# Where three chunks of modulation products run: in the delta scan, or behind the first feed-forward layer in another bank

## The chip, the cores and the metric

One Trainium2 chip, one core. The metric is the time of one execution on the device in microseconds (us). Engines: TensorE (PE, matmuls; PEld its weight loads), VectorE (DVE), ScalarE (ACT), GpSimd (POOL) and SyncE (SP, which issues nearly all loads).

## What is computed

A stack of two blocks on 256 tokens of width 1024, batch 1, all in float32. The first block has two layers: a hybrid mixer (gated delta rule and attention) with a feed-forward layer, then a conformer convolution with a feed-forward layer. The second block (`second_block`) follows on its output. What matters here is the modulation of the first block's layers:

```python
def ada_terms(cond, w_mod, b_mod):
    m = jax.nn.silu(cond) @ w_mod + b_mod          # (D,) @ (D, 6 D)
    return jnp.split(m, 6, axis=-1)

for layer in range(DEPTH):                          # DEPTH = 2
    sh1, sc1, gt1, sh2, sc2, gt2 = ada_terms(c[:, None, :], w_mod[layer], b_mod[layer])
    a = modulate(rms_norm(h, g_mix_pre[layer]), sh1, sc1)
    ...
    h = h + gt1 * rms_norm(y, g_mix_post[layer])
    f = swiglu_ffn(modulate(rms_norm(h, g_ffn_pre[layer]), sh2, sc2), w_ffn_in[layer], w_ffn_out[layer])
    h = h + gt2 * rms_norm(f, g_ffn_post[layer])
```

Layer 1's six vectors are needed at different times: the first three (shift, scale, gate of the mixer) around the conformer, the last three (shift, scale, gate of the feed-forward) only after the conformer.

## The kernel before

Every weight goes through a ring of four slots of 3072 columns in SBUF. `ORDERED` lists all chunks in the order of their use; `SLOT_OF` gives the slot, `BEFORE` the chunk that a load has to wait for, `DONE` the semaphore and count that tell that a chunk is used. SP walks this list in order: wait until the chunk's slot is free, issue the load, next. A load that has to wait holds back all that follow.

**Modulation.** `w_mod` of each layer is cut into 16 chunks of 384 output columns (1536 KB each), `MODS` lists all 32. `mod_products(m)` (its matmuls are L815) does 8 matmuls of 128x384 for one chunk, in four column groups of PE; the page counts each of them twice (x16). They accumulate in `mod_acc`, part of PSUM bank 7, over a whole run of chunks. `MOD_RUNS` has three runs: chunks 0 to 5, 6 to 15 (both layer 0) and 16 to 31 (layer 1). At the end of a run ACT copies `mod_acc` to SBUF (L1790), PE turns it into columns with the selection matrix (`mod_columns`, L823, into `mod_out`, also bank 7), DVE adds the bias (`mod_take`, L2248) and `mod(layer, vectors)` makes gains, shifts and the columns `pcol` of the post-norms.

**The delta scan.** It has four steps of short dependent matmuls (L1109, `per_head`) with DVE work between them. To fill the time PE has generators of other work and a table `GAPS`, written out by hand: at each named place of the scan (`pause(name)`) every letter advances one generator: M one chunk of modulation products, S attention scores (L1179), T transposes of attention weights (L776), V attention outputs (L1200), N the normalisation of weights (ACT and DVE only). ACT and DVE walk the same table with their own generators, so the letters set the order on three engines. `SLOT_OF` uses three of the four slots there. Chunks 6 to 31 all run in the scan or just ahead of it; then the four chunks of the mixer's output projection (`hyb_o`) follow, split into a high and a low part by ACT (L1985) and DVE (L2619), and `out_rows_parts` (L905) multiplies them into banks 4 to 7 (`Y`: token tile 0 in banks 4 and 5, tile 1 in 6 and 7). It waits until DVE has read the scan's last banks (L2689).

**The first feed-forward layer** (`ffn("ffn0", ...)`) runs 22 blocks: input products (L955, L956), then row products (L990) into `Y`. At its end the rows of tile 0 are finished before those of tile 1. `post(1)` (DVE L2342 to L2350, ACT L1674 to L1683) normalises and adds to `h`, `norm_stats(3)` and `norm_scale(3)` make the next norm, PE transposes it (`norm(3)`, 16 transposes, L789), ACT (L1636) and DVE (L2300) apply gain and shift.

**The conformer.** `glu_pair(c)` (L832) makes value and gate of one block of 128 features from one `conf_i` chunk (1024 KB); ACT reads the gate (L2048), DVE the value (L2735). Eight pairs, then the convolution: `conv_taps`, which writes banks 4 to 7, and `conv_sum`.

```python
GAPS = {
...
    "ds1": "SMTM", "ks2": "VMNM", "vn2": "SMTM", "os2": "MNS", "ds2": "TMNM", "oi2": "SMVM", "ks3": "TMNM", "vn3": "MTM",
    "os3": "MV",
}
MOD_RUNS = ((0, MOD_CTX), (MOD_CTX, NMOD), (NMOD, NMODS))
```

Of the kernel before, what the change touches and what calls it, by code (L numbers as in the profile page):

```python
# [25 lines left out]
ALU = mybir.AluOpType  # L26
ACT = mybir.ActivationFunctionType
# [3 lines left out]
P = 128  # L31
# [27 lines left out]
MOD_C = 384  # L59
# [20 lines left out]
MODS = [("mod0", _j) for _j in range(NMOD)] + [("mod1", _j) for _j in range(NMOD)]  # L80
ORDERED = MODS[:MOD_CTX] + HYB_CHUNKS + MODS[MOD_CTX:] + [("hyb_o", _j) for _j in range(4)]
_rest = len(ORDERED)
ORDERED += [(_name, _j) for _name, _chunks, _ in STREAM[4:] for _j in range(_chunks)]
CHUNK = {key: _n for _n, key in enumerate(ORDERED)}

# [117 lines left out]
for _name, _c in HYB_CHUNKS:  # L203
# [17 lines left out]
    "qk": "MSMM", "p5": "M", "q5": "M", "p6": "M", "q6": "SM", "vn0": "TMNSM", "ds0": "TMN", "ks1": "SMV", "vn1": "TMN",  # L221
    "ds1": "SMTM", "ks2": "VMNM", "vn2": "SMTM", "os2": "MNS", "ds2": "TMNM", "oi2": "SMVM", "ks3": "TMNM", "vn3": "MTM",
    "os3": "MV",
# [128 lines left out]

MOD_RUNS = ((0, MOD_CTX), (MOD_CTX, NMOD), (NMOD, NMODS))
STRIP = 32
# [6 lines left out]
def build(nc, w, w_mod1, cols_in, rows_in, consts_in, b_out_in, c_bd_in, glu_in, b_in, x_in, ctx_in, out):  # L361
    ctx = ExitStack()
    w = {**w, "mod1": w_mod1}
    with ctx:
# [113 lines left out]

        mod_acc, mod_out = psum[:, 3584:3584 + MOD_C], psum[:, 3968:4096]

        mod_ev = (z_t[:, 0:MOD_C], arena[:, 15712:15712 + MOD_C], arena[:, 15712:15712 + MOD_C])
        ident, ones = const("ident"), const("ones")
# [228 lines left out]
        def _(sp):  # L711
# [21 lines left out]
            for name, n, _ in STREAM[3:]:  # L733
# [20 lines left out]
                for j in range(head, n):  # L754
                    wait_used(c0 + j)
                    load(c0 + j, name, j)
            for t in range(TT):
                for half in range(2):
                    cols_of = slice(half * 512, half * 512 + 512)
                    sp.wait_ge(h_ready, 10 + 2 * t + half + 1)  # L760
                    sp.dma_start(out[t * P:(t + 1) * P, cols_of], h[:, t, cols_of]).then_inc(stored, 16)
# [4 lines left out]
        def _(pe):  # L766
# [37 lines left out]
            def mod_products(m):  # L804

                run = [n for n, (m0, m1) in enumerate(MOD_RUNS) if m0 <= m < m1][0]
                (m0, m1), c = MOD_RUNS[run], CHUNK[MODS[m]]
                if m == m0 and run:  # L810
                    pe.wait_ge(mod_taken, run)
                wait_ring(c)
                for k in range(KT):
                    q, at = 32 * (k % 4), STRIP * k + 15 - (m - m0)
                    last = mm(mod_acc[q:q + 32, :], cond[:, at:at + 32], slot(c)[:, k * MOD_C:(k + 1) * MOD_C],  # L815
                              start=(m == m0 and k < 4), stop=(m == m1 - 1 and k >= 4))
                last.then_inc(ring_used, 1)

            def mod_columns(run):

                pe.wait_ge(mod_rows, run + 1)
                for b in range(3):
                    last = mm(mod_out[:, 32 * b:32 * b + 32], mod_ev[run][:, b * P:(b + 1) * P], sel, start=True, stop=True)  # L823
                last.then_inc(mod_sel, 1)
# [525 lines left out]
            ffn("ffn0", NF, 1)  # L1350


            norm(3)
            c0 = FIRST["conf_i"]
            def glu_pair(c):
# [6 lines left out]
            def conv_taps(n):  # L1362


                c, use = CONV_PE[n], USE["taps31"][n]
                wait_read(pe, USE["conf_i"][c])
                pe.wait_ge(taps_ready, 2 * n + 2)
                wait_free(pe, use)
# [231 lines left out]
        def _(act):  # L1600
# [438 lines left out]

            norm_stats(3)  # L2040
            act.wait_ge(mod_ready, 3)
            norm_evac(3)
# [193 lines left out]
        def _(dve):  # L2236
# [4 lines left out]
            def mod_take(run):  # L2241
# [4 lines left out]
                for c in range(1 if run else 2):  # L2246
                    rows_of = mod_out[:, 0:96].rearrange("p (b m) -> p m b", b=3)[:, 16 * c:16 * c + m1 - m0, :]
                    ch.mark(tt(modT[:, layer, tiles, c].rearrange("p (m b) -> p m b", b=3), rows_of,  # L2248
                               col("b_mod")[:, 48 * layer:48 * layer + 48][:, tiles].rearrange("p (m b) -> p m b", b=3), ALU.add))
# [3 lines left out]
            def mod(layer, vectors):  # L2253
                m = modT[:, layer, :, :]
                early, late = 0 in vectors, 5 in vectors
                gain = lambda name: col(name)[:, KT * layer:KT * layer + KT]
# [7 lines left out]
                for i, at, name, c in todo:  # L2264

                    ch.mark(stt(ngain[:, i, :], m[:, at + 8:at + 16, c], 1.0, gain(name), ALU.add, ALU.mult))
                    ch.mark(v.tensor_copy(nshift[:, i, :], m[:, at:at + 8, c]))
                if late:
                    ch.mark(tt(pcol[:, 2 * layer, :], m[:, 16:24, 0], gain("g_mix_post"), ALU.mult))
                    ch.mark(tt(pcol[:, 2 * layer + 1, :], m[:, 40:48, 0], gain("g_ffn_post"), ALU.mult))  # L2270
# [440 lines left out]
            for n in range(6, KT):  # L2711
                hyb_o_weights(n)
            mod(1, (0, 1, 2, 3, 4, 5))
            row_diag(1)
# [11 lines left out]
            norm_evac(3)  # L2726
            row_diag(2)
            dve.wait_ge(margins, 2)
            dww = col("conf_dw_w").rearrange("p (b k) -> p b k", k=CONF_K)
# [577 lines left out]
```

## Time and profile before

| | us |
|---|---|
| median of 3 runs | 1325.77 (1323.71 to 1328.1) |
| the profiled execution | 1321.74 |
| its span | 1319.9 |
| PE busy in it | 1250.8 (95%) |
| DVE / ACT / POOL busy | 908.4 / 542.6 / 125.2 |
| mean granted clock of PE | 0.982 |
| read from HBM | 223.81 MB, 170 GB/s over the span |

The profile is of one execution. A row of a timeline gives start, duration (of all the instructions that it merges), engine, line, operation, what is written from what, the number of instructions and, in brackets, the idle time of the engine before it with what ended it. Matmuls are pipelined, so the duration of one overlaps the start of the next. The granted clock is a share of 2.4 GHz; 0.50 is 1.2 GHz.

### The profile page before, as it was taken

The page shows a single profiled execution, that of the slowest core. Times are in us where ns is not written, and L with a number is a line of the kernel's source. Part 1 is how long each engine was busy: PE and PEld are TensorE (multiplying, and loading weights), DVE is VectorE, ACT ScalarE, POOL GpSimd, SP SyncE. Part 2 cuts the span into 40 slices and gives each one's busy share as a digit, 9 for nine tenths or more (in the row PEclk, how much of TensorE's full clock was granted, in tenths as well). Part 3 has the DMA queues.
Part 4 walks back from the last instruction along what each step waited for, and adds up shares of the span by engine and source line. Part 5 has one row for each costly group of instructions (what it writes and reads, how often), then busy time and mean ns, then how long its engine had stood idle before and what let it go on. Part 6 is the DMA issues. An engine that isn't in the chain of part 4 may idle for free. (4 is left out here: it accounts for less than half of the span.)

```text
span 1319.9 us, 19518 instructions
## 1 busy us (share of the span) xinstructions
PE 1250.8 (95%) x7382; PEld 996.3 (75%) x7382; DVE 908.4 (69%) x1554; ACT 542.6 (41%) x906; POOL 125.2 (9%) x165
## 2 busy tenths in 40 slices
PE   4999979999999998999999999899999999899997
PEld 1777646557888887884688888777878987788886
DVE  0547896458777775795777777389977545777776
ACT  2664266345444444015543334311226534544443
POOL 0062022000000002000000000245530000000000
PEclk8999989999999998999999999899999999999999
DMA  9322377995655542421455555124333433555551
GB/s 390 138 81 96 136 288 287 365 344 185 238 184 184 186 158 72 157 97 47 164 220 191 191 191 191 65 96 150 138 105 136 144 112 128 192 191 184 184 182 54
DMA packets 24951, 225.80 MB, mean 171 GB/s; under 512 B 2738, under 2 KB 2866, under 8 KB 4659
## 3 DMA queue, kind: packets, MB, share of 16 engines
q1 hardware_dynamic: 23328, 220.31, 45.7%
q10 hardware_dynamic: 1554, 4.56, 1.0%
q8 instruction: 46, 0.75, 0.2%
q14 instruction: 23, 0.18, 0.0%
HBM read 223.81 MB, written 1.05 MB: 170 GB/s over the span
## 5 line engine op out<-in xcount | busy, mean ns | idle before, releaser
L955 PE MATMUL psum<-aT_r,arena_r 128*128 128x512 f32 x920 | 327.5, 398 | 1.4 <-DVE arena_r L2363 1.0
L2363 DVE TENSOR_TENSOR arena_r<-ring,arena_r 128x1024 fp32r<-128x1024 f32 x188 | 220.4, 1221 | 98.2 <-ACT arena_r L1700 98.1
L956 PE MATMUL psum<-aT_r,arena_r 128*128 128x256 f32 x920 | 258.1, 281 | 0.0
L1700 ACT ACTIVATE arena_r<-ring 128x1024 fp32r<-128x1024 f32 x188 | 186.9, 1051 | 143.6 <-PE psum L990 133.3
L990 PE MATMUL psum<-arena_r 128*128 128x512 f32 x876 | 213.4, 392 | 0.0
L832 PE MATMUL psum<-aT,ring 128*128 128x256 f32 (+1 forms) x896 | 211.0, 394 | 0.0
L955 PEld LDWEIGHTS psum<-aT_r,arena_r 128*128 128x128 f32 x920 | 172.8, 188 | 43.9 <-issue 2.0
L832 PEld LDWEIGHTS psum<-aT,ring 128*128 128x128 f32 x896 | 170.2, 192 | 38.9 <-issue 17.5
L990 PEld LDWEIGHTS psum<-arena_r 128*128 128x128 f32 x876 | 159.5, 188 | 34.8
L956 PEld LDWEIGHTS psum<-aT_r,arena_r 128*128 128x128 f32 x920 | 173.7, 189 | 2.6
L1712 ACT ACTIVATE nrm<-nrm 128x256 f32<-128x256 f32 x76 | 31.8, 418 | 165.1 <-DVE nrm L2381 161.9
L815 PE MATMUL psum<-ring,cond 128*32 128x384 f32 x512 | 52.1, 532 | 23.0 <-DMA consts<-in_consts 12.4
L2749 DVE SCALAR_TENSOR_TENSOR arena<-arena,cols 128x256 f32<-128x256 f32 x120 | 52.8, 482 | 1.9
L815 PEld LDWEIGHTS psum<-ring,cond 128*32 128x32 f32 x512 | 14.4, 114 | 50.1 <-issue 34.5
L2381 DVE TENSOR_REDUCE nrm<-psum 128x256 f32<-128x512 f32 x73 | 49.8, 683 | 0.0
L2398 DVE TENSOR_TENSOR nrm<-nrm 128x256 f32<-128x256 f32 x76 | 32.3, 426 | 22.1 <-ACT nrm L1712 16.1
L2388 DVE TENSOR_REDUCE nrm<-psum 128x256 f32<-128x512 f32 x42 | 29.1, 692 | 20.4 <-PE psum L956 20.4
L2488 DVE SCALAR_TENSOR_TENSOR arena<-arena,cols 128x512 f32<-128x512 f32 (+1 forms) x48 | 35.3, 763 | 1.1
L1441 PE MATMUL psum<-aT_r,ring_r 128*128 128x256 f32 x120 | 33.8, 282 | 0.0
L2406 DVE TENSOR_TENSOR arena_r<-nrm,arena_r 128x256 fp32r<-128x256 f32 x73 | 31.0, 425 | 2.5
L3167 POOL MEMSET arena<- 128x24 f32 x1 | 0.1, 123 | 315.3 <-DVE nrm L2290 315.3
L863 PE MATMUL psum<-ring,arena 128*128 128x512 f32 x64 | 29.8, 623 | 0.0
(550 smaller groups left out, 1900.8 us busy)
## 6 DMA issues: line engine op xcount, KB each, us to landing
ring<-in_w_ffn SPq DMA_DIRECT2D x44, 1536.0 KB, 6.7
ring<-in_w_mod SPq DMA_DIRECT2D x32, 1536.0 KB, 8.6
ring<-in_w_ff SPq DMA_DIRECT2D x32, 1024.0 KB, 4.8
ring<-in_w_in_g SPq DMA_DIRECT2D x8, 1536.0 KB, 6.5
ring<-in_w_conf_i SPq DMA_DIRECT2D x8, 1024.0 KB, 5.0
ring<-in_w_hyb_f SPq DMA_DIRECT2D x4, 1536.0 KB, 6.8
ring<-in_w_in_a SPq DMA_DIRECT2D x4, 1536.0 KB, 6.6
ring<-in_w_in_b SPq DMA_DIRECT2D x4, 1536.0 KB, 6.3
```

The source lines that it names most:

```text
L815: last = mm(mod_acc[q:q + 32, :], cond[:, at:at + 32], slot(c)[:, k * MOD_C:(k + 1) * MOD_C], start=(m == m0 and k < 4), stop=(m == m1 - 1 ...
L832: last = mm(bank(use)[:, out_at:out_at + rhs(k).shape[1]], weights[:, k * P:(k + 1) * P], rhs(k), start=(k == 0), stop=(k == KT - 1))
L955: mm(bank(use).rearrange("p (a t) -> p a t", a=2), hi, x_both[:, :, k, :], start=(k == 0), stop=False)
L956: last = mm(bank(use)[:, T:2 * T], lo, x_hi[:, k, :], start=False, stop=(k == KT - 1))
L990: last = mm(Y[:, t, half * 512:half * 512 + 512], act_part, w_part[:, half * 512:half * 512 + 512], start=(isinstance(i, int) and j == 0 a ...
L1441: mm(bank(use)[:, 0:T], w_lo_b[:, at], gate_x_hi[:, k, :], start=False, stop=False)
L1700: fn(out_hi[2] if last_out else w_hi[j % 2][:, at], slot(c)[:, at], ACT.Copy).then_inc(split_hi, 1)
L2363: tt(lo, slot(c)[:, at], hi.bitcast(F32), ALU.subtract).then_inc(split_ready, 1)
L2381: summed = v.reduce_sum(g_sum[:, j % 2, :], bank(gate).rearrange("p (a t) -> p t a", a=2), axis=AXX)
L2398: tt(h_tmp, sg[:, j % 2, :], u_sum if parts == 3 else sg[:, j % 2, :], ALU.mult).then_inc(h_step, 1)
L2488: last = stt(cv[:, b, 0:n, :], cin[:, b, 0:n, k:k + T], taps[:, b, k:k + 1], cv[:, b, 0:n, :], ALU.mult, ALU.add)
L2749: last = stt(cc[:, c, :], cu[:, c, k:k + T], dww[:, c, k:k + 1], cc[:, c, :], ALU.mult, ALU.add)
```

## The change

The last three chunks of layer 1's products (29, 30, 31) become a run of their own, `MOD_LATE` on. Their loads come behind the last chunk of `ffn0` in SP's order, ahead of `conf_i`, so the four `hyb_o` loads move up by three places, and all later chunks sit three slots further round the ring. Their products run behind `ffn0` and ahead of `norm(3)`, into bank 4 instead of bank 7; PE waits there until DVE and ACT have read tile 0 of `Y` (`y_gained`, `post_ss`). ACT copies the sum behind `norm_stats(3)` and ahead of `norm_evac(3)`, PE's `mod_columns(3)` stands behind `norm(3)`, DVE's `mod_take(3)` and `mod(1, (3, 4, 5))` behind `row_diag(2)`. `mod(1, ...)` is split: vectors 0 to 2 stay where all six were. `conv_taps(0)` waits until bank 4 has been read (`mod_taken`). In `GAPS` one M goes from `ks3` and one from `vn3`; since the third run is three chunks shorter, the M left in `vn3` now does the selection matmuls, and that of `os3` nothing.

```diff
-ORDERED = MODS[:MOD_CTX] + HYB_CHUNKS + MODS[MOD_CTX:] + [("hyb_o", _j) for _j in range(4)]
+MOD_LATE = NMODS - 3
+ORDERED = MODS[:MOD_CTX] + HYB_CHUNKS + MODS[MOD_CTX:MOD_LATE] + [("hyb_o", _j) for _j in range(4)]
 _rest = len(ORDERED)
-ORDERED += [(_name, _j) for _name, _chunks, _ in STREAM[4:] for _j in range(_chunks)]
+for _name, _chunks, _ in STREAM[4:]:
+    ORDERED += [(_name, _j) for _j in range(_chunks)]
+    if _name == "ffn0":
+        ORDERED += MODS[MOD_LATE:]
...
-    "ds1": "SMTM", "ks2": "VMNM", "vn2": "SMTM", "os2": "MNS", "ds2": "TMNM", "oi2": "SMVM", "ks3": "TMNM", "vn3": "MTM",
+    "ds1": "SMTM", "ks2": "VMNM", "vn2": "SMTM", "os2": "MNS", "ds2": "TMNM", "oi2": "SMVM", "ks3": "TMN", "vn3": "MT",
...
-MOD_RUNS = ((0, MOD_CTX), (MOD_CTX, NMOD), (NMOD, NMODS))
+MOD_RUNS = ((0, MOD_CTX), (MOD_CTX, NMOD), (NMOD, MOD_LATE), (MOD_LATE, NMODS))
...
+        mod_banks = [(mod_acc, mod_out)] * 3 + [(psum[:, 2048:2048 + MOD_C], psum[:, 2432:2560])]
-        mod_ev = (z_t[:, 0:MOD_C], arena[:, 15712:15712 + MOD_C], arena[:, 15712:15712 + MOD_C])
+        mod_ev = (z_t[:, 0:MOD_C], arena[:, 15712:15712 + MOD_C], arena[:, 15712:15712 + MOD_C], z_t[:, 0:MOD_C])
...
+                if name == "ffn0":
+                    for m in range(MOD_LATE, NMODS):
+                        wait_used(CHUNK[MODS[m]])
+                        load(CHUNK[MODS[m]], *MODS[m])
...
             ffn("ffn0", NF, 1)
+            pe.wait_ge(y_gained, 4 + 2)
+            pe.wait_ge(post_ss, 4 + 2)
+            for m in range(MOD_LATE, NMODS):
+                mod_products(m)
             norm(3)
+            mod_columns(3)
...
+                if n == 0:
+                    pe.wait_ge(mod_taken, 4)
                 pe.wait_ge(taps_ready, 2 * n + 2)
...
             norm_stats(3)
+            act.wait_ge(ring_used, DONE[CHUNK[MODS[NMODS - 1]]][1])
+            fn(mod_ev[3], mod_banks[3][0], ACT.Copy).then_inc(mod_rows, 1)
             act.wait_ge(mod_ready, 3)
             norm_evac(3)
...
-            mod(1, (0, 1, 2, 3, 4, 5))
+            mod(1, (0, 1, 2))
...
             norm_evac(3)
             row_diag(2)
+            mod_take(3)
+            mod(1, (3, 4, 5))
```

PE at the end of the scan, its third and fourth step, before. L815 are modulation products, L1109 the scan's own matmuls, L776 attention transposes, L823 the selection matmuls, L1200 attention outputs, L841 the row broadcast, L905 the output projection:

```order
L1109 MATMUL psum<-yT,arena 128x128 x8
L776 MATMUL psum<-consts,arena 128x128 x8
L815 MATMUL psum<-ring,cond 32x384 x16
L1109 MATMUL psum<-arena,aT 128x128 x8
L815 MATMUL psum<-ring,cond 32x384 x8
L776 MATMUL psum<-consts,arena 128x128 x8
L815 MATMUL psum<-ring,cond 32x384 x8
L1109 MATMUL psum<-yT,arena 128x128 x8
L823 MATMUL psum<-sel,arena 128x32 x3
L1200 MATMUL psum<-ring,tok 64x256 x8
L1109 MATMUL psum<-arena 128x128 x8
L841 MATMUL psum<-diag,consts 128x512 x2
```

The same stretch with the change (lines moved by 9: L824 are the modulation products, L832 the selection):

```order
L1118 MATMUL psum<-yT,arena 128x128 x8
L785 MATMUL psum<-consts,arena 128x128 x8
L824 MATMUL psum<-ring,cond 32x384 x8
L1118 MATMUL psum<-arena,aT 128x128 x8
L832 MATMUL psum<-sel,arena 128x32 x3
L785 MATMUL psum<-consts,arena 128x128 x8
L1118 MATMUL psum<-yT,arena 128x128 x8
L1209 MATMUL psum<-ring,tok 64x256 x8
L1118 MATMUL psum<-arena 128x128 x8
L850 MATMUL psum<-diag,consts 128x512 x2
```

Three of the four chunks (8 matmuls each) are gone, and the selection stands two places further ahead, in front of the attention transposes.

PE at the end of `ffn0`, before: row products (L990), the norm's transposes (L789), the conformer's input products (L832):

```order
L990 MATMUL psum<-arena_r 128x512 x12
L990 MATMUL psum<-decay_r,z_r 128x512 x6
L789 MATMUL psum<-consts,nrm 128x128 x16
L832 MATMUL psum<-aT,ring 128x256 x112
L1374 MATMUL psum<-arena,yT 128x259 x4
```

And with the change:

```order
L999 MATMUL psum<-arena_r 128x512 x12
L999 MATMUL psum<-decay_r,z_r 128x512 x6
L824 MATMUL psum<-ring,cond 32x384 x24
L798 MATMUL psum<-consts,nrm 128x128 x16
L832 MATMUL psum<-sel,z 128x32 x3
L841 MATMUL psum<-aT,ring 128x256 x112
L1390 MATMUL psum<-arena,yT 128x259 x4
```

The 24 late products stand between the last row products and the transposes, the three selection matmuls between the transposes and the conformer.

## Rows read from the trace of the kernel before

**Rows 1.** The page, part 1: busy us, share of the span and instructions of PE.

```profile
PE 1250.8 (95%) x7382; PEld 996.3 (75%) x7382; DVE 908.4 (69%) x1554; ACT 542.6 (41%) x906; POOL 125.2 (9%) x165
```

**Rows 2.** Timeline of PE, end of the scan: start, us, engine, line, operation [idle before <-releaser].

```profile
260.62 2.07 PE L815 MATMUL psum<-ring,cond 128*32 128x384 f32 x16 [2.04 <-DMA ring<-in_w_mod]
...
276.02 1.50 PE L815 MATMUL psum<-ring,cond 128*32 128x384 f32 x16 [0.24 <-DMA ring<-in_w_mod]
...
279.91 1.50 PE L815 MATMUL psum<-ring,cond 128*32 128x384 f32 x16 [0.41 <-DMA ring<-in_w_mod]
281.34 1.09 PE L776 MATMUL psum<-consts,arena 128*128 128x128 f32 x8
284.25 1.50 PE L815 MATMUL psum<-ring,cond 128*32 128x384 f32 x16 [1.82 <-DMA ring<-in_w_mod]
...
287.57 0.75 PE L823 MATMUL psum<-sel,arena 128*128 128x32 f32 x6
...
294.53 1.16 PE L905 MATMUL psum<-ring_r,decay_r 128*128 128x512 f32 x4 [0.63 <-issue]
```

**Rows 3.** Windows in the scan: busy us, instructions, then granted clock, DMA share, GB/s.

```profile
260.00:280.00 20.00, 18.73 (x160) 10.98 (x164) 6.67 (x11) 5.13 (x12) 0.00 (x0) 0.91 0.99 382
262.00:264.00 2.00, 2.00 (x14) 1.38 (x7) 0.00 (x0) 0.00 (x0) 0.00 (x0) 0.50 1.01 430
```

**Rows 4.** Timeline of PE, from the end of the first feed-forward layer.

```profile
509.15 1.52 PE L990 MATMUL psum<-decay_r,z_r 128*128 128x512 f32 x6
515.00 3.67 PE L789 MATMUL psum<-consts,nrm 128*128 128x128 f32 x16 [4.33 <-DVE nrm L2290]
518.58 9.77 PE L832 MATMUL psum<-aT,ring 128*128 128x256 f32 x39
```

**Rows 5.** Windows behind the first feed-forward layer, columns as in rows 3.

```profile
514.00:516.00 2.00, 1.00 (x5) 1.00 (x6) 1.51 (x7) 1.62 (x4) 0.00 (x0) 0.50 0.20 77
...
520.00:522.00 2.00, 2.00 (x9) 1.70 (x8) 2.00 (x1) 1.15 (x1) 2.00 (x3) 0.79 0.00 0
```

**Rows 6.** Timeline of ACT, end of the scan.

```profile
282.03 1.08 ACT L1904 ACTIVATE ring<-psum 128x512 f32<-128x512 f32 x2 [5.22 <-PE psum L776]
285.81 0.49 ACT L1790 ACTIVATE arena<-psum 128x384 f32<-128x384 f32 x1 [2.70 <-PE psum L815]
286.76 1.06 ACT L1985 ACTIVATE ring_r<-ring 128x1024 fp32r<-128x1024 f32 x1 [0.45 <-DMA ring<-in_w_hyb_o]
```

**Rows 7.** Timeline of DVE, end of the scan.

```profile
287.85 1.23 DVE L2619 TENSOR_TENSOR ring_r<-ring,ring_r 128x1024 fp32r<-128x1024 f32 x1 [6.62 <-ACT ring_r L1985]
...
291.33 0.20 DVE L2248 TENSOR_TENSOR mod<-psum,cols 128x48 f32<-128x48 f32 x1
...
293.74 0.69 DVE L2689 TENSOR_TENSOR o<-o,psum 128x512 f32<-128x512 f32 x1
```

**Rows 8.** Timeline of ACT, next norm and the first two gates of the conformer.

```profile
517.92 1.93 ACT L1636 ACTIVATE aT<-psum,nshift,ngain 128x256 f32<-128x256 f32 x4 [2.26 <-PE psum L789]
...
526.87 0.47 ACT L2048 ACTIVATE arena<-psum,cols 128x256 f32<-128x256 f32 x1 [5.72 <-PE psum L832]
533.77 0.47 ACT L2048 ACTIVATE arena<-psum,cols 128x256 f32<-128x256 f32 x1 [6.43 <-PE psum L832]
```

**Rows 9.** Timeline of DVE, its first work in the conformer.

```profile
527.44 0.48 DVE L2735 SCALAR_TENSOR_TENSOR arena<-psum,cols,arena 128x256 f32<-128x256 f32 x1 [5.45 <-ACT arena L2048]
```

**Rows 10.** SP's loads from 470 to 560: issues (first and last start), time to landing.

```profile
L717 SPq DMA_DIRECT2D ring<-in_w_conf_i x8: 327/328/331, 476.8 to 547.6; - x8
...
DMA to landing us min/median/max: 4.8/5.0/7.7
```

**Rows 11.** Timeline of PE, behind the second feed-forward layer.

```profile
839.98 3.68 PE L789 MATMUL psum<-consts,nrm 128*128 128x128 f32 x16 [4.25 <-DVE nrm L2290]
```

**Rows 12.** PE's first transposes (timeline), and a window there (columns as in rows 3).

```profile
25.78 3.67 PE L789 MATMUL psum<-consts,ybuf 128*128 128x128 f32 x16 [0.77 <-DVE ybuf L2290]
```

```profile
28.00:32.00 4.00, 2.88 (x23) 1.47 (x21) 0.00 (x0) 0.41 (x1) 0.00 (x0) 0.84 1.01 421
```

More of the change, by code:

```diff
@@ L814, in mod_products @@
                     q, at = 32 * (k % 4), STRIP * k + 15 - (m - m0)
-                    last = mm(mod_acc[q:q + 32, :], cond[:, at:at + 32], slot(c)[:, k * MOD_C:(k + 1) * MOD_C],
+                    last = mm(mod_banks[run][0][q:q + 32, :], cond[:, at:at + 32], slot(c)[:, k * MOD_C:(k + 1) * MOD_C],
                               start=(m == m0 and k < 4), stop=(m == m1 - 1 and k >= 4))
@@ L822, in mod_columns @@
                 for b in range(3):
-                    last = mm(mod_out[:, 32 * b:32 * b + 32], mod_ev[run][:, b * P:(b + 1) * P], sel, start=True, stop=True)
+                    last = mm(mod_banks[run][1][:, 32 * b:32 * b + 32], mod_ev[run][:, b * P:(b + 1) * P], sel, start=True, stop=True)
                 last.then_inc(mod_sel, 1)
@@ L2246, in mod_take @@
                 for c in range(1 if run else 2):
-                    rows_of = mod_out[:, 0:96].rearrange("p (b m) -> p m b", b=3)[:, 16 * c:16 * c + m1 - m0, :]
+                    rows_of = mod_banks[run][1][:, 0:96].rearrange("p (b m) -> p m b", b=3)[:, 16 * c:16 * c + m1 - m0, :]
                     ch.mark(tt(modT[:, layer, tiles, c].rearrange("p (m b) -> p m b", b=3), rows_of,
@@ L2254, in mod @@
                 m = modT[:, layer, :, :]
-                early, late = 0 in vectors, 5 in vectors
+                early, late, gate = 0 in vectors, 3 in vectors, 2 in vectors
                 gain = lambda name: col(name)[:, KT * layer:KT * layer + KT]
@@ L2267, in mod @@
                     ch.mark(v.tensor_copy(nshift[:, i, :], m[:, at:at + 8, c]))
+                if gate:
+                    ch.mark(tt(pcol[:, 2 * layer, :], m[:, 16:24, 0], gain("g_mix_post"), ALU.mult))
                 if late:
-                    ch.mark(tt(pcol[:, 2 * layer, :], m[:, 16:24, 0], gain("g_mix_post"), ALU.mult))
                     ch.mark(tt(pcol[:, 2 * layer + 1, :], m[:, 40:48, 0], gain("g_ffn_post"), ALU.mult))
```

## The prediction

> **What bounds the kernel now.** I read the page first: TensorE (PE) is busy for 95% of the span [rows 1], so an edit pays only where it takes PE work away, closes a hole in it, or raises its clock. Then I read PE in order of time at the two places that the diff touches. At the end of the delta scan [rows 2] the reader is to see that the last three products of modulation chunks (L815, x16 each) start after waits of 0.24, 0.41 and 1.82 us for their own weights; the windows [rows 3] show why: the 16 DMA engines are 0.99 busy at 382 GB/s. At the end of the first feed-forward layer [rows 4] PE stands still for 4.33 us between its last row products and the transposes of the next norm, and the windows show that the granted clock is 0.50 in 514 to 516, that is the level of 1.2 GHz instead of 2.4 [rows 5]. So the change takes work from a place where it waits for DMA to one where PE has nothing to do. Last I read ACT and DVE at both places, to see what else would hold the end of each [rows 6, 7, 8].
>
> **The scan, by PE.** The output projection starts at 294.53 [rows 2]. What leaves the stretch ahead of it is three products at 1.43 us each (279.91 to 281.34, start to next start), 4.3 us, and their three waits, 2.5 us; the selection matmuls (L823) stay and only move ahead. The freed M of the last step does nothing. PE alone would come out 6.8 us sooner.
>
> **The scan, by ACT and DVE.** PE is not alone. The projection cannot start before DVE has read the last bank of the scan: L2689 at 293.74 takes 0.69 and ends at 294.43, PE starts at 294.53 [rows 2, 7]. DVE works without a break from 287.85, where it had waited 6.62 us for ACT's copy of the first projection weights (L1985) [rows 7]; ACT did that copy at 286.76, behind the mod copy (L1790, 285.81, waiting 2.70 for PE) and 0.45 us of DMA [rows 6]. In the changed kernel the mod copy is done three chunks sooner, so ACT goes to L1985 right behind its two turned attention banks (L1904, now 282.03, 1.08 us). These come sooner by two products and their waits (2 x 1.43 + 0.24 + 0.41 = 3.5) and later by the selection matmuls that now stand before them (0.68, from the 0.75 of x6 at 287.57): at 279.2. Then 279.2 + 1.08 + 1.06 = 281.3 for DVE's first subtraction instead of 287.85, 6.5 us sooner. The weights are there: the first projection chunk (1024 KB for 1536) now takes the place in SP's queue of a load that PE had by 276.02, the second that of one it had by 279.91, the third that of one it had by 284.25 [rows 2]. DVE's 6.5 us is the smaller of the two, so I take **-6.5 us** (ends: -6.8, and -3.1, which is what rival 2 leaves of it). What follows to the feed-forward layer keeps its spacing, since each load and each wait of it is released by something that moves along.
>
> **Behind the feed-forward layer: the products.** PE's last row products end at 509.15 + 1.52 = 510.67 and the transposes start at 515.00 because DVE's norm is ready then [rows 4]. Three products of 1.43 end at 514.97. They wait for the bank of the first token tile only, which was read before the second tile's products were through. Cost **0** (ends: 0 and the whole 4.3, if something keeps them from starting in the gap). Their three loads stand in SP's queue where three conf_i loads stood, from 476.8 on [rows 10], so they are in the ring 20 us before use. ACT's copy of 128x384 (0.49, as L1790 in the scan) falls in its 2.26 us of waiting for the transposes [rows 6, 8]. The bias add (0.20 for L2248 in the scan, rows 7), three more such small operations and a tick on DVE fall in the 5.45 us in which it waits for the first gate [rows 9]; if that cover were gone, five at 0.20 would cost 1.0. The selection matmuls stand ahead of the first conformer product: 0.68 us, of which about half lies where PE would wait for the evacuation anyway: **+0.3** (ends 0 and 0.7).
>
> **Behind the feed-forward layer: the clock.** Before, the first pair of conformer products starts at 518.58 and its gate is read at 526.87, 8.3 us; the next pair takes 526.87 to 533.77, 6.9 [rows 4, 8]. At full clock 1.4 us come back. The 16 transposes took 3.67 us [rows 4]; eight at full clock take 1.09 (the x8 at 281.34, rows 2), and the second tile's eight are on the path: about 0.5 more. **-1.9** if the clock holds, 0 if it falls all the same, and I take -1.9: the only thing that PE did before the clock fell was to stand still for 4.33 us, and the new products fill that stretch. The same gap of 4.25 us stands ahead of the norm after the second feed-forward layer [rows 11]; it is unchanged and serves as the control.
> Between the new products and the conformer's stand the 16 transposes. Before, the clock stayed at 0.50 while they ran and rose only in 520 to 522, behind 518.58 where the conformer's products begin [rows 4, 5]; at the start of the kernel it rose in 28 to 32 with little but transposes running since 25.78 [rows 12].
> The Trainium skill (TensorE: Matmul & The Clock Gate, Part 4: PE-mode transpose) says that a transpose does not count as PE work for the clock as other matmuls do. By that rule the transposes would let the clock fall, only later, and the clock term would be near 0 instead of -1.9. The trace is divided on it: the first of the two stretches agrees, the second speaks against it.
>
> **Sum.** -6.5 + 0 + 0.3 - 1.9 = **-8.1 us**. The profiled execution took 1321.74 (span 1319.9), the median of the runs shown is 1325.77, 4.0 above it, and the runs are up to 2.3 from their median. Against the profiled execution the sum gives 1313.6; against the median, which I forecast, **1317.7**. A measurement of this kernel can tell about 0.3%, 4 us, from no change.
>
> **Rivals.**
> 1. The clock falls anyway in front of the conformer (the transposes and the short waits between them do it). Then -6.5 + 0.3 = -6.2: 1319.6. For it: the transposes do not keep PE full, since DVE delivers the second tile's half behind the first's. Against: there is hardly an empty us left. (The rule of the Trainium skill named above is of this rival's side.)
> 2. The scan gains less, because its last steps lose their filler and PE has holes between them: after a wait of 2.04 us at 260.62 the clock was 0.50 in 262 to 264 [rows 2, 3]. If that happens where the projection starts, some 7 us of it run at half speed, 3.4 us: -4.7, 1321.1. Against: the longest wait that I count there is under 1 us.
> 3. The work is moved, not hidden: PE pays the 4.3 us in full behind the layer (a wait in front of the products) and the clock gives nothing back. -6.5 + 4.3 + 0.3 = -1.9: 1323.9.
> 4. The change does not do what it says: the scan ends when it did, since its waits for DMA hid other waits of the same length (attention's normed weights, the state update), and behind the layer the clock falls as before. 0: 1325.8.
> 5. Slower: the ring. Late products hold three of its four slots, so conf_i chunks 1 to 3 are issued at 512 to 515 instead of from 476.8 on. PE needs chunk 1 at about 525, and each further one 6.9 us later. A conf_i load landed 5.0 us after its issue in the median and 7.7 at worst [rows 10]. From 13 us on PE waits; to lose the 8.1 us won and 4 more, chunk 1 must take 25 us, three times the worst: 1330. Against it: even three loads one behind the other at 7.7 are all in time, and nothing else is loaded then.
>
> **How the numbers follow.** Forecast 0.50; rival 1 0.17; rival 2 0.12; rival 3 0.08; rival 4 0.05; rival 5 0.08. Faster by over 0.3% (below 1321.8): the forecast, rival 1 and half of rival 2, 0.73; within 0.3%: the other half, rivals 3 and 4, 0.19; slower: 0.08. The range runs from 1313.3 (both gains at their ends, -8.7, and 3.7 for the scatter of a median and of places where the clock falls by chance) to 1323.5, which takes in rivals 1 and 2 with scatter and leaves rivals 3, 4 and 5 mostly outside.
>
> **What would show it.** In the changed profile: no product waits for DMA after about 274; the projection's first matmul at 288.0 (right: 287.5 to 288.5); DVE's first subtraction of projection weights near 281.3; 24 products (three x16) right after the last row products and the transposes after them without idle; clock 1.00 there, and first and second gate 6.9 us apart from the start of the pair; the twin gap after the second layer still 4.2 us with a clock of 0.50. Wrong, if the projection starts later than 290, if the late products wait for y_gained or the ring, if the clock in the windows ahead of the conformer is 0.50, or if the conformer's products wait for ring<-in_w_conf_i.

## The result, and the profile after

| | before | changed |
|---|---|---|
| runs made together, median us | 1324.74 (1323.58 to 1328.1, 4 runs) | 1311.72 (1309.85 to 1313.82, 4 runs) |
| the profiled execution | 1321.74 | 1312.18 |
| its span | 1319.9 | 1310.3 |
| mean granted clock of PE | 0.982 | 0.985 |

The ratio is 0.9909 [0.989, 0.9928]: faster by 0.9%, and by more than forecast; 1311.72 lies 1.6 us below the range. Later both kernels ran more often. Over all their runs before has a mean of 1323.6 us (83 runs, standard error 0.3) and the changed kernel one of 1313.4 (16 runs, 0.4): **-10.2 us**. The two spans differ by 9.6.

The page of the changed kernel, parts 1 and 2 (for before see [rows 1]):

```profile
PE 1246.6 (95%) x7388; PEld 992.4 (76%) x7388; DVE 908.5 (69%) x1557; ACT 542.9 (41%) x907; POOL 125.2 (10%) x165
...
PEclk8999979999999999999999999899999999999999
```

PE is busy for 4.2 us less with six matmuls more, which points to the clock.

**The scan.** Timeline of PE in the changed kernel, as [rows 2] (L824 are the products, L832 the selection, L785 the attention transposes, L914 the projection):

```profile
271.08 1.50 PE L824 MATMUL psum<-ring,cond 128*32 128x384 f32 x16
...
275.37 1.50 PE L824 MATMUL psum<-ring,cond 128*32 128x384 f32 x16
276.79 2.05 PE L1118 MATMUL psum<-arena,aT 128*128 128x128 f32 x16
278.68 0.75 PE L832 MATMUL psum<-sel,arena 128*128 128x32 f32 x6
...
288.67 1.17 PE L914 MATMUL psum<-ring_r,decay_r 128*128 128x512 f32 x4 [0.71 <-DVE o L2708]
```

The window there, as [rows 3]: busy us of PE, PEld, DVE, ACT, POOL, then granted clock, DMA share, GB/s.

```profile
262.00:288.00 26.00, 24.64 (x206) 16.32 (x206) 13.76 (x24) 14.01 (x26) 0.00 (x0) 1.00 0.78 296
```

ACT and DVE there, as [rows 6, 7], each a timeline of its own:

```profile
279.94 1.09 ACT L1920 ACTIVATE ring<-psum 128x512 f32<-128x512 f32 x2 [1.30 <-PE psum L785]
280.91 1.06 ACT L2001 ACTIVATE ring_r<-ring 128x1024 fp32r<-128x1024 f32 x1
```

```profile
282.01 1.22 DVE L2638 TENSOR_TENSOR ring_r<-ring,ring_r 128x1024 fp32r<-128x1024 f32 x1 [1.43 <-ACT ring_r L2001]
...
287.88 0.69 DVE L2708 TENSOR_TENSOR o<-o,psum 128x512 f32<-128x512 f32 x1
```

No product waits for its weights any more from 264 on, and the DMA engines have room (0.78 instead of 0.99). The projection starts at 288.67 instead of 294.53, **5.9 us sooner**, and it waits for the engine that the prediction named: DVE's last read ends at 288.57. DVE's subtraction is 5.84 sooner, and from it to the projection it is 6.66 us, before 6.68.

**Behind the first feed-forward layer.** Timeline of PE, as [rows 4]:

```profile
503.38 1.52 PE L999 MATMUL psum<-decay_r,z_r 128*128 128x512 f32 x6
504.83 4.08 PE L824 MATMUL psum<-ring,cond 128*32 128x384 f32 x48
509.23 1.09 PE L798 MATMUL psum<-consts,nrm 128*128 128x128 f32 x8 [0.32 <-DVE nrm L2309]
510.65 1.09 PE L798 MATMUL psum<-consts,nrm 128*128 128x128 f32 x8 [0.34 <-DVE nrm L2309]
511.58 0.75 PE L832 MATMUL psum<-sel,z 128*128 128x32 f32 x6
512.28 3.91 PE L841 MATMUL psum<-aT,ring 128*128 128x256 f32 x17
```

Windows, as [rows 5], and ACT's first two gates, as [rows 8]:

```profile
504.00:509.00 5.00, 4.91 (x52) 1.85 (x51) 3.65 (x8) 3.85 (x10) 0.00 (x0) 1.00 0.33 88
509.00:512.00 3.00, 2.44 (x21) 2.20 (x21) 2.48 (x7) 1.82 (x6) 0.95 (x4) 1.00 1.00 396
512.00:516.00 4.00, 4.00 (x21) 3.56 (x21) 3.96 (x7) 2.63 (x4) 4.00 (x3) 1.00 1.01 424
```

```profile
519.46 0.47 ACT L2066 ACTIVATE arena<-psum,cols 128x256 f32<-128x256 f32 x1 [4.82 <-PE psum L841]
526.37 0.47 ACT L2066 ACTIVATE arena<-psum,cols 128x256 f32<-128x256 f32 x1 [6.43 <-PE psum L841]
```

The products fill the hole to 0.32 us. From the last row products to the transposes it is 5.85 us, before also 5.85: they cost nothing. The clock stays at 1.00 through products and transposes; the gate is read 7.2 us after the first pair's start (before 8.3) and the next 6.9 later. The conformer's products wait for no load.

**The twin gap**, behind the second layer, as [rows 11], with its window: as before, 4.25 us of idle and a clock near 0.50.

```profile
830.61 3.67 PE L798 MATMUL psum<-consts,nrm 128*128 128x128 f32 x16 [4.25 <-DVE nrm L2309]
```

```profile
828.00:834.00 6.00, 3.39 (x16) 3.27 (x16) 4.50 (x12) 3.61 (x9) 1.37 (x4) 0.54 0.00 0
```

**Where the 9.6 us of the spans went.** Starts of the same instructions on PE (the bias rows are the one-row matmuls that open the convolution, L857, now L866):

| | before | changed | difference | of it here |
|---|---|---|---|---|
| projection | 294.53 | 288.67 | -5.86 | -5.9 |
| norm after the first layer | 515.00 | 509.23 | -5.77 | +0.1 |
| bias rows | 608.86 | 601.45 | -7.41 | -1.6 |
| norm after the second layer | 839.98 | 830.61 | -9.37 | -2.0 |
| end of the span | 1319.9 | 1310.3 | -9.6 | -0.2 |

The third line is the clock term. The fourth was not expected: nothing was changed there. Windows there, of before:

```profile
613.00:617.00 4.00, 4.00 (x7) 1.66 (x6) 0.89 (x6) 3.17 (x6) 0.00 (x0) 0.58 0.02 4
651.00:654.00 3.00, 3.00 (x16) 2.99 (x15) 2.88 (x8) 2.75 (x7) 0.00 (x0) 0.51 0.10 34
```

and of the changed kernel, over both places (they lie 7 to 9 us sooner there):

```profile
601.00:660.00 59.00, 55.52 (x227) 34.23 (x226) 46.09 (x108) 34.65 (x63) 0.00 (x0) 1.00 0.46 164
```

Before, the clock fell to its lower level at 613 and at 651, at 613 out of full work, at 651 just behind a wait of 2.19 us for DVE. In the changed kernel it did at neither, though PE waits 2.18 us there too (at 641.15).

One pair of profiles is a small base for this table. Two more profiles of the changed kernel and one more of before were taken later (experiments 1, 11 and 12). The means of two against three are -6.5 at the projection, then -0.4, -1.1, -2.8 and -0.1, together -10.9. So the clock term is -0.5 to -1.6, by the profile of before that one takes, and the unforeseen term -2.0 or more.

### The profile page after: what moved, and what is told of

Same layout as the page of the kernel before. It is cut to its first block and busy times, and to the rows that moved or that the text cites. A ratio compares the mean times of both kernels' runs of the same rounds, so it can differ in the third digit from the quotient of the medians.

```text
span 1310.3 us, 19537 instructions
## 1 busy us (share of the span) xinstructions
PE 1246.6 (95%) x7388; PEld 992.4 (76%) x7388; DVE 908.5 (69%) x1557; ACT 542.9 (41%) x907; POOL 125.2 (10%) x165
## 5 line engine op out<-in xcount | busy, mean ns | idle before, releaser
L841 PE MATMUL psum<-aT,ring 128*128 128x256 f32 (+1 forms) x896 | 209.7, 393 | 0.0
L841 PEld LDWEIGHTS psum<-aT,ring 128*128 128x128 f32 x896 | 169.3, 190 | 38.3 <-issue 17.2
L824 PE MATMUL psum<-ring,cond 128*32 128x384 f32 x512 | 53.7, 548 | 20.6 <-DMA consts<-in_consts 12.5
L824 PEld LDWEIGHTS psum<-ring,cond 128*32 128x32 f32 x512 | 14.9, 118 | 49.0 <-issue 36.9
L1560 PE MATMUL psum<-yT,ring 128*128 128x256 f32 x128 | 28.9, 379 | 0.0
```

The lines of the kernel that those rows point to most:

```text
L824: last = mm(mod_banks[run][0][q:q + 32, :], cond[:, at:at + 32], slot(c)[:, k * MOD_C:(k + 1) * MOD_C], start=(m == m0 and k < 4), stop=(m ...
L841: last = mm(bank(use)[:, out_at:out_at + rhs(k).shape[1]], weights[:, k * P:(k + 1) * P], rhs(k), start=(k == 0), stop=(k == KT - 1))
L1560: last = mm(bank(use)[:, (br % 2) * T:(br % 2 + 1) * T], slot(c)[:, wat:wat + P], ys[br][:, k, :], start=(k == 0), stop=(k == 3))
```

## The experiments

Besides the forecast ("it fills a hole, so the clock holds") two rivals were open: that the saving in the scan comes from the loads or from PE's work, and that what is won behind the layer comes from elsewhere than the clock.

**1. Before once more**, no edit.

> The unchanged kernel once more, for a second profile of it and for the granted clock of its runs. Theory (the term for the clock was right, but the profiled execution of before was one of its quickest, with the clock down at fewer places than usual): the runs scatter over 3 us or more and the slower ones have the lower mean clock; the projection starts within 1.5 us of 294.5 in the profile, the norm behind the first feed-forward layer within 1.5 of 515.0. Rival (the scan's waits for DMA scatter): the projection's start moves by 3 us or more between the two profiles. Ratio 1.000.

1324.57 (12 runs), ratio 1.0004 [0.9989, 1.002]. The time is as expected, the profile is not. Its span was 1324.1, 4.2 more than that of the profile shown before, with the same program: its projection starts at 296.69, its norm behind the layer at 518.70 (both expected within 1.5 of the first profile, they lie 2.2 and 3.7 behind it), and its clock was 0.978. So two profiles of one kernel can differ by 4 us, and a term of 1 us can't be read from one pair of spans, only from the stretch where it arises. Even that is not always the same: from the transposes to the bias rows it is 92.76 us here and 93.86 in the first profile. Timeline of its PE, then windows:

```profile
518.70 3.32 PE L789 MATMUL psum<-consts,nrm 128*128 128x128 f32 x16 [4.33 <-DVE nrm L2290]
522.28 12.97 PE L832 MATMUL psum<-aT,ring 128*128 128x256 f32 x59 [0.26 <-DVE aT L2300]
```

```profile
518.00:522.00 4.00, 3.30 (x16) 3.09 (x16) 2.92 (x8) 1.70 (x4) 1.47 (x4) 0.57 0.04 15
522.00:526.00 4.00, 3.74 (x18) 3.33 (x18) 3.71 (x4) 2.83 (x5) 4.00 (x5) 1.00 0.00 0
```

The clock was back at 1.00 by 522, before the first conformer product, so the same gap of 4.33 us cost less here. Until then only the 16 transposes had run.

**2. The late products left out** of the changed kernel (six narrow ones stay for the semaphores):

```diff
+                    if run < 3:
                         last = mm(mod_banks[run][0][q:q + 32, :], ...)
+                    elif k < (4 if m == m0 else 1):
+                        last = mm(mod_banks[run][0][q:q + 32, 0:32], cond[:, at:at + 32], slot(c)[:, 0:32], start=True, stop=True)
```

> The changed kernel with the products of the three late chunks left out: of 24 matmuls of 128x384 only 6 of 32 columns remain, loads, waits, copies and selection stay, so the last three modulation vectors are partly missing from the result. Theory (the late products cost nothing and hold the clock up): less work, but slower than the changed kernel by 1.6 to 1.9 us, about 1313.5 in the median, the clock at 0.50 around the next norm, PE idle 3.5 to 4.3 us there; the projection starts at 288.7 as in the changed kernel. Rival (late products are paid in part): quicker than the changed kernel by up to 4.3 us.

1317.54 (9 runs), ratio 0.9955 [0.9938, 0.9973]; with 18 matmuls less it is about 4 us **slower** than the changed kernel. Timeline of its PE, then a window:

```profile
506.11 1.52 PE L1002 MATMUL psum<-decay_r,z_r 128*128 128x512 f32 x6
507.56 0.38 PE L828 MATMUL psum<-ring,cond 128*32 128x32 f32 x12
511.95 3.68 PE L798 MATMUL psum<-consts,nrm 128*128 128x128 f32 x16 [4.02 <-DVE nrm L2312]
515.42 1.33 PE L835 MATMUL psum<-sel,z 128*128 128x32 f32 x6
```

```profile
511.00:521.00 10.00, 9.04 (x33) 8.15 (x34) 8.71 (x19) 5.18 (x10) 7.21 (x10) 0.50 0.68 279
```

The hole is back, the clock falls, and the selection takes 1.33 us instead of 0.75. From the transposes to the bias rows it is 96.05 us, in the changed kernel 92.22. The direction is as expected, the size is twice the 1.6 to 1.9 us expected: the clock stays at 0.50 for 10 us, in the first profile of before for 7 (514 to 521). Why it stays low for longer is open.

**3. Only a filler**: before, nothing moved, with 24 more matmuls of 128x384 in the gap (`fill`): behind the waits that the change has there, into bank 4, results unused.

```diff
             ffn("ffn0", NF, 1)
+            fill(FIRST["conf_i"], 6)
             norm(3)
```

> The kernel before with nothing moved, but 24 extra matmuls of 128x384 on the first conf_i chunk into bank 4, never read, where the changed kernel has its late products. Theory: the idle 4.33 us are filled at no cost and the clock holds: -1.6 to -1.9 us against before in the profile behind the layer, ratio 0.9986; more, up to -3.6, if the places at 613 and 651 where the clock fell before go too. Rival (the gain behind the layer comes from something else that moved, such as the ring's slots or the loads): 0, or up to +1 from the extra work.

1320.49 (12 runs), ratio 0.9984 [0.9966, 1.0001]; in means -2.5 us, with a standard error of 0.9. Work was added and the kernel got no slower, rather faster. Timeline of its PE, then its window:

```profile
511.19 4.08 PE L1036 MATMUL psum<-ring,cond 128*32 128x384 f32 x48
515.59 1.09 PE L789 MATMUL psum<-consts,nrm 128*128 128x128 f32 x8 [0.32 <-DVE nrm L2297]
```

```profile
510.00:519.00 9.00, 7.82 (x72) 4.25 (x71) 7.13 (x16) 5.93 (x15) 1.58 (x4) 1.00 0.11 29
```

From its transposes to the bias rows it is 92.22 us, to the hundredth that of the changed kernel (before 93.86 and 92.76). So what that stretch gains is the clock's, 1.6 us or 0.5 by the profile of before, and the moved work with its selection costs 0.0 there. Its profile still has the falls around 613 and 651.

**4. Three products out of the scan, their loads stay**: before, with one narrow matmul for each of the last three chunks.

> The kernel before with the products of the last three chunks left out (one matmul of 32 columns for each of them remains, on its slot), while their loads stay where they were, ahead of hyb_o. Theory (the end of the scan is paced by DMA: it waits for those loads whether or not it multiplies): PE still waits for the loads, longer than before, up to 1.8 us more in total, and the projection starts 1.4 to 2.5 us sooner, at 292 to 293, not at 288.7. Rival (PE's products are what the change takes away, 4.3 us): the projection starts at 290.2 or sooner.

1324.29 (12 runs), ratio 1.0001 [0.9986, 1.0015]: nothing, where 1.4 to 2.5 us were expected, and its projection starts at 295.57. Timeline of its PE, then of ACT and of DVE:

```profile
277.86 0.25 PE L819 MATMUL psum<-ring,cond 128*32 128x32 f32 x2 [1.19 <-DMA ring<-in_w_mod]
...
281.56 0.25 PE L819 MATMUL psum<-ring,cond 128*32 128x32 f32 x2 [1.46 <-DMA ring<-in_w_mod]
...
285.25 0.25 PE L819 MATMUL psum<-ring,cond 128*32 128x32 f32 x2 [2.42 <-DMA ring<-in_w_mod]
```

```profile
287.80 1.06 ACT L1988 ACTIVATE ring_r<-ring 128x1024 fp32r<-128x1024 f32 x1 [1.77 <-DMA ring<-in_w_hyb_o]
```

```profile
288.89 1.22 DVE L2622 TENSOR_TENSOR ring_r<-ring,ring_r 128x1024 fp32r<-128x1024 f32 x1 [7.06 <-ACT ring_r L1988]
```

Of the 3.75 us taken from the three products 2.6 come back as longer waits for their loads ([rows 2] had 0.24, 0.41, 1.82). The clock also fell here, in 286 to 290 (0.61), which slowed PE. But that did not set the projection's start: ACT waits 1.77 us for the first projection chunk, and DVE then works without a break from 288.89 to the projection. The scan before was paced by its loads.

**5. Three loads out of the scan, their products stay**: the changed kernel, with three chunks' worth of products on constants at the old places (`ks3` "TMNM", `vn3` "MTM", ACT's copy behind them).

> The changed kernel with three chunks' worth of extra products put back where the three chunks were in the scan (same letters as before, the 24 matmuls of 128x384 read the constants instead of a ring chunk and add to the layer's sums, so part of the modulation is wrong), and no loads for them. With products_out_loads_stay it makes the other corner of the square: there products left and the loads stayed, and nothing was won. Theory (both pace the scan's end, the loads first and PE's products right behind them): the projection starts at 292.0 to 293.0, about 2.5 us ahead of before (295) and 3.8 behind the changed kernel. Rival (only the loads count, PE has room): at 288.5 to 289.5. Rival 2 (only the products count): 294.5 or later.

1315.35 (7 runs), ratio 0.9936 [0.9912, 0.9959]. The end of the scan, PE:

```profile
285.30 0.75 PE L832 MATMUL psum<-sel,arena 128*128 128x32 f32 x6
...
291.68 1.17 PE L914 MATMUL psum<-ring_r,decay_r 128*128 128x512 f32 x4
```

The projection lies 3.0 us behind that of the changed kernel; in means of the runs it is 2.6, with a standard error of 1.4. The start of the projection alone is a weak measure: over the seven profiles here whose scan is that of the changed kernel it lies between 287.67 and 291.37. The stretch from the last product that stays to the projection is a better one. It is 13.30 to 13.32 us in all seven, 20.24 and 21.29 in the two profiles of before, 20.39 with the products out (experiment 4) and 16.84 here. Of a scan gain of 6.9 or more, loads out with products kept gives about half and products out with loads kept gives nothing: both have to go, and the loads have to go first.

**6. The late products in bank 7** (`mod_acc`) instead of bank 4; they must then wait until all of `Y` is read.

```diff
-        mod_banks = [(mod_acc, mod_out)] * 3 + [(psum[:, 2048:2048 + MOD_C], psum[:, 2432:2560])]
+        mod_banks = [(mod_acc, mod_out)] * 4
-            pe.wait_ge(y_gained, 4 + 2)
-            pe.wait_ge(post_ss, 4 + 2)
+            pe.wait_ge(y_gained, 4 + 4)
+            pe.wait_ge(post_ss, 4 + 4)
```

> The changed kernel with the late products in bank 7 as before, so that they wait until both token tiles of Y have been read. Theory (the other bank is what lets them start at once): they start at 506.4 instead of 504.8, end at about 510.8 and push the transposes of the second tile (510.65) back by 1 us: 0.8 to 1.3 us slower than the changed kernel, 1.6 us of idle time ahead of them, clock still at 1.00. Rival (the bank does not matter, the norm's chain ends last anyway): 0. Rival 2 (the idle 1.6 us lets the clock fall): 2 us slower or more.

1314.80 (6 runs), ratio 0.9932 [0.9913, 0.9951]. Timeline of its PE:

```profile
505.65 1.52 PE L999 MATMUL psum<-decay_r,z_r 128*128 128x512 f32 x6
508.90 4.08 PE L824 MATMUL psum<-ring,cond 128*32 128x384 f32 x48 [1.73 <-DVE ybuf L2364]
...
515.40 1.97 PE L841 MATMUL psum<-aT,ring 128*128 128x256 f32 x8
```

The other bank saves this wait of 1.73. From the last row products to the conformer it is 9.75 us here, 8.90 with bank 4: 0.9 us, since the transposes then have no wait of their own. Over the runs it is 1.1, within their scatter. The expectation (0.8 to 1.3) holds. Its profile has the falls again, at 609 and 647.

**7. Four chunks late** (`MOD_LATE = NMODS - 4`, one M less in `ks3`) and **8. six late** (four M's less in `GAPS`, one of them empty).

> Four chunks late instead of three (the M of ks3 goes too). Theory (the scan is paced by its loads, at about 2 us of gain for each chunk, and the gap behind the layer holds three products): scan 1.5 to 2 us sooner, behind the layer 5.7 us of products against 4.4 of gap, 1.0 to 1.4 later, so 0 to 1 us quicker than the changed kernel. Rival (with three out the scan is no longer paced by its loads): the projection starts 0.7 us sooner at most and the kernel is 0.5 to 1 us slower. Rival 2 (the fourth late chunk holds the ring's last slot and conf_i comes late): PE waits for ring<-in_w_conf_i, 2 us slower or more.

> Six chunks late instead of three, so that the ring's turn of three slots in the scan stays as it is. Theory (behind three the scan is bound by PE, the gap holds three products, and the ring's four slots hold four late chunks): the 9.14 us wait of ACT that four late had is gone; the projection starts 2 to 5 us ahead of the changed kernel; behind the layer PE waits for the fifth and sixth chunk and then for conf_i, and pays 4.3 us of products and 2 to 6 of waits: 1 to 6 us slower than the changed kernel in all. Rival (loads out of the scan are worth about 2 us each wherever they go): as quick or quicker.

Four: 1325.13 (12 runs), ratio 1.0011 [0.9999, 1.0024], the whole gain lost, where up to 1 us more was expected. Six: 1320.36 (12 runs), ratio 0.9983 [0.9969, 0.9998], in means 7.7 us behind the changed kernel, where 1 to 6 were expected. With four the late work costs 0.9 us (row products to transposes 6.75 us instead of 5.85); most is lost elsewhere. ACT of that kernel, then its SP, at the start of the first feed-forward layer:

```profile
319.38 1.06 ACT L1716 ACTIVATE arena_r<-ring 128x1024 fp32r<-128x1024 f32 x1 [9.14 <-DMA ring<-in_w_ffn]
```

```profile
296.27 0.33 SPq L722 DMA_DIRECT2D ring<-in_w_hyb_o  x1
312.80 0.33 SPq L722 DMA_DIRECT2D ring<-in_w_ffn  x1
```

The ring is dealt out by turn, and while the scan runs by three slots. Three chunks less is one whole turn, so every load up to the end of the first feed-forward layer meets the slot that it met before; four chunks less shift the turn, and the layer's second load comes 22.3 us after the projection's start instead of 12.1 (300.76 in the changed kernel). Six, two whole turns, has no such wait. Its projection starts at 286.74, 1.9 us sooner than with three, which is less than such starts scatter. It loses behind the layer instead. PE of that kernel:

```profile
502.80 5.37 PE L824 MATMUL psum<-ring,cond 128*32 128x384 f32 x64
513.42 2.79 PE L824 MATMUL psum<-ring,cond 128*32 128x384 f32 x16 [5.25 <-DMA ring<-in_w_mod]
517.10 1.50 PE L824 MATMUL psum<-ring,cond 128*32 128x384 f32 x16 [0.89 <-DMA ring<-in_w_mod]
```

Four chunks are in the ring's four slots in time; the fifth can be loaded only when the first is used, and PE stands for 5.25 us.

**9. The twin gap filled as well**: the changed kernel, with the filler of experiment 3 ahead of `norm(5)`.

> The changed kernel with 24 extra matmuls of 128x384 (on the first in_a chunk, into bank 4, never read) in the twin gap of 4.25 us behind the second feed-forward layer. Theory (filling an idle stretch with any products holds the clock): the clock stays at 1.00 in 830 to 845 of its profile, first block behind the norm 1.4 us sooner, in all 1.6 to 3 us quicker than the changed kernel. Rival (at the first gap it was the moved work, not the clock): 0.

1313.66 (6 runs), ratio 0.993 [0.9914, 0.9946], no different from the changed kernel beside it (1313.70). Its profile shows the clock at 1.00 there:

```profile
830.00:845.00 15.00, 14.06 (x72) 12.17 (x70) 2.94 (x7) 3.38 (x8) 7.86 (x14) 1.00 0.06 11
```

From this norm to the next layer's it is 281.62 us instead of 282.69, so about 1.1 us are won there. That is less than the 1.6 to 3 expected, and six runs don't show it. Here too a wait of 0.53 stays ahead of the next product.

**10. Eight more matmuls** behind the late products, as a mere delay of about 1.1 us, to see whether the falls at 613 and 651 hang on the time at which PE arrives.

> The changed kernel with 8 more matmuls of 128x384 (on constants, into bank 5, never read) behind the late products: everything behind the layer comes 1.0 to 1.4 us later. Theory (the falls of the clock around 613 and 651 in before and their absence in the changed kernel follow from where the timeline happens to stand, not from what was moved): in this kernel's profile a clock of 0.50 stands in 600 to 655 at least once, and its runs lie 1 to 4 us above those of the changed kernel, with more scatter. Rival (the falls went away for good with the change): no 0.50 in 500 to 660 and 1.0 to 1.4 us.

1313.38 (6 runs), ratio 0.992 [0.990, 0.994]. A window of its PE at the bias rows:

```profile
608.00:611.00 3.00, 3.00 (x5) 1.27 (x4) 0.93 (x7) 2.08 (x4) 0.00 (x0) 0.50 0.00 0
```

The clock fell again at 608 and at 645, and from the bias rows to the norm it is 231.1 us as before, not 229.2. The runs do not show it: with the delay and the falls they should lie 3 us above those of the changed kernel, and their mean is the same (1313.3, standard error of the difference 0.8). The profiled execution was the slowest of the six (1316.11), so one profile doesn't tell how often an execution of this kernel has the falls.

**11 and 12. The changed kernel again**, beside the others.

> The changed kernel once more, on the same chip and beside the same runs of before as the three below. Theory (half of the gain is the scan's loads, half the clock): ratio 0.990 to 0.992, mean clock of its runs 0.984 to 0.988 against 0.976 to 0.982 of before; in a second profile the projection starts 5 to 8 us ahead of before and no clock of 0.50 stands between 500 and 660. Rival (the 13 us are partly a lucky few runs): ratio 0.993 or more.

> The changed kernel a third time, as the neighbour of the three above and for the median over all its runs. Theory: ratio 0.990 to 0.993; projection at 287.5 to 291.5, no clock of 0.50 in 500 to 655 in most profiles.

1313.70 (6 runs), ratio 0.993 [0.9915, 0.9946], and 1314.24 (6 runs), ratio 0.9929 [0.9908, 0.9949]. The first lies where its rival said, 0.993 or more: the first four runs were in part lucky. Both profiles have no fall at 613 or 651, and projections at 288.51 and 290.01.

## Why the prediction was wrong where it was, step by step

The forecast was -8.1 from a base of 1325.77; the first four runs gave 1311.72, 6.0 us below it. That divides into three about equal parts. **The base**: the three runs shown were on the high side; the mean of before is 1323.6, 2.2 less. **The effect**: -10.2 instead of -8.1, 2.1. **The luck of four runs**: 1311.7 where the mean of sixteen is 1313.4, 1.7. With the mean of 16 runs the range would just have held the time (1313.4 against 1313.3), but as it was made it did not. The prediction even noted that the profiled execution was 4.0 us below the median, and took the median of three as the base without widening the range downwards for it.

- **The scan, -6.5: right.** Measured -5.9 between the two profiles, and the last product that stays came 1.1 us later in the changed one, from which the rest gains 6.9 (8.0 against the second profile of before). DVE's subtraction was expected near 281.3 and came at 282.01, the projection at 288.0 and came at 288.67, both by that later start. The reason given, that the place waits for DMA, is confirmed by experiments 4 and 5: products out alone wins nothing.
- **The late products, 0: right** (5.85 us before and after; experiment 3). That they need the other bank is right as well, and worth 0.9 (experiment 6).
- **The selection, +0.3: a little too much.** The stretch is the same to the hundredth without it (experiment 3): its 0.7 us take the place of a wait of 0.53 for the evacuation. Shown: 0.0.
- **The clock behind the layer, -1.9: right in place and kind**, measured -1.6 against the first profile of before and only -0.5 against the second, so too much in size. The mechanism is shown from both sides: the products out, and the fall is back (experiment 2); the filler alone, and it is gone (experiment 3).
- **The step that failed** is the one sentence that put "places where the clock falls by chance" into the range's scatter: the sum has no term for the clock behind the conformer. The falls at 613 and 651 were in the trace of before and were taken as constant. Both are missing in all three profiles of the changed kernel, and between the two profiles compared that is 2.0 us, between the means of profiles 2.8. The second fault is the base, 2.2 too high.

What decides these falls stays open. Of the fourteen profiles here nine have both falls, a few us earlier or later with the kernel's own times, and five have neither. With them are both of before, its filler (3) and its products out (4), but also five kernels with late work: 5, 6, 7, 8 and 10. Without them are the three of the changed kernel, 2 and 9. So the moved work doesn't forbid the falls, and mere lateness doesn't bring them: experiment 10, 1.3 us later than the first profile at the bias rows, had both, the third profile of the changed kernel, 2.3 us later, had none, and experiment 2, 6.6 later, neither. From the bias rows to the norm behind the second layer it is 229.2 to 229.3 us in the five and 230.9 to 232.9 in the nine. That the change makes the falls rarer over many executions is not shown by profiles of single ones. It fits that the runs' mean clock rose by 0.004 (0.980 in the median of before's runs, 0.984 in the changed kernel's): among runs of before the time falls by about 0.83 us for each 0.001, which makes 3.3 us, near the -1.6 and the -2.0 together.

Of the rivals, the first (the clock falls all the same) and the second (the scan's holes let it fall) did not happen: 1.00 in both places. By the rule of the Trainium skill (TensorE: Matmul & The Clock Gate, Part 4: PE-mode transpose), as the prediction read it, the clock would have fallen behind the 16 transposes; the traces of the changed kernel and of experiment 3 do not agree. The third is refuted by the 5.85, the fourth by the projection. The fifth, the ring, did not come with three chunks: the conf_i chunks 1 to 3 were issued as late as it said (at 506.4 to 509.3, with everything 5.9 us sooner), and no conformer product waited. The ring is what took the gain with four and with six, though by other ways than the one described: the turn of the slots, and a fifth chunk for four slots.

## What to carry to other kernels

Work with its own loads is cheap to move when it leaves a stretch that waits for DMA and enters a hole in which TensorE waits for another engine; price the hole twice, once for the work that fits in it and once for the clock that it costs. Before moving n chunks of a ring, count turns: here a number that wasn't a whole turn (four), and one that was more than the ring has slots (six), delayed or starved loads far from the edit. And take a base from more than three runs where the forecast argues about 2 us.

## What was not expected of the hardware

- **Added work that costs nothing and gives time back**: 24 matmuls (4.08 us of PE) in a gap of 4.33 us left the kernel at a ratio of 0.9984 [0.9966, 1.0001], in means 2.5 us quicker with a standard error of 0.9.
- **The clock can fall while PE is busy.** In before PE was busy for 5.00 of 5.00 us from 608 to 613 and the clock fell at 613; in experiment 10 it was busy for 6.00 of 6.00 from 602 to 608, and it fell just ahead of 608. In the changed kernel the same instructions ran at 1.00. In all nine profiles with this fall it came 2 to 5 us after the start of the bias rows, eight matmuls over a single partition (timeline of before). They stand in the five profiles without it too, and whether they matter for it was not tried:

```profile
608.86 3.69 PE L857 MATMUL psum<-tok,consts 1*128 1x512 f32 x8
```

- **The scatter is mostly the clock's.** Over 83 runs of before the time lay between 1318.8 and 1329.0. In the 79 of them whose clock is on record the mean clock lay between 0.975 and 0.986 and goes with the time at a correlation of -0.84. One run decides nothing under 5 us here.
